# The first projections in quarters of the weights' rows, with the modulation of the next quarter between their products

## What is computed

```
mod   = silu(c) @ w_mod + b_mod          # sa, ca, ga, sm, cm, gm = split(mod, 6)
mod_c = silu(c_ctx) @ w_mod + b_mod      # only sa_c, ca_c are used
h_c = rmsnorm(ctx, w) * (1 + ca_c) + sa_c
k_c, v_c = h_c @ w_in[:, K_OFF:P_OFF]    # K_OFF 1024, P_OFF 3072
h = rmsnorm(x, w) * (1 + ca) + sa
q, k, v, u = h @ w_in[:, 0:4096]         # 1024 columns each; u goes to the pooling branch
# attention over [k; k_c], gates from w_in[:, 4096:8192], pooling of u, w_o, MLP, second block
```

## Time and profile before

| | |
|---|---|
| median of 3 runs | 2528.29 us (2527.92 to 2528.49) |
| time of the profiled execution | 2526.87 us |
| its span, first to last instruction | 2525.1 us |
| PE busy | 2384.4 us, 94% |
| DVE busy | 1372.6 us, 54% |
| ACT busy | 1120.2 us, 44% |
| mean granted TensorE clock | 0.978 |

### The profile page before, as it was taken

One profiled execution on the slowest core, in us unless ns is written; L12 is line 12 of the kernel. 1 busy time (PEld: TensorE's weight loads), 2 busy tenths in 40 slices (PEclk: granted clock), 3 DMA queues, 4 the chain that ended last, 5 costly groups with the idle time before them and its releaser, 6 DMA issues.

```text
span 2525.1 us, 31441 instructions
## 1 busy us (share of the span) xinstructions
PE 2384.4 (94%) x12376; PEld 1882.2 (75%) x12376; DVE 1372.6 (54%) x2020; ACT 1120.2 (44%) x1638; POOL 64.6 (3%) x87
## 2 busy tenths in 40 slices
PE   4699999999989998999999999999999999999998
PEld 1277887666666666888888888878888887788976
DVE  0044444666544545555555555575477555559874
ACT  2155444444433335444444444445455454456553
POOL 2000000110000000000000000000000000000000
PEclk9689999999999998999999999999999999999999
DMA  9955664666678885655655555655543566542233
GB/s 332 364 156 162 198 192 160 237 242 233 233 251 303 286 308 173 186 188 191 185 187 191 186 186 187 192 168 183 183 134 118 174 227 205 174 140 84 86 133 117
DMA packets 243187, 494.52 MB, mean 196 GB/s; under 512 B 7928, under 2 KB 8288, under 8 KB 241808
## 3 DMA queue, kind: packets, MB, share of 16 engines
q1 hardware_dynamic: 239232, 476.08, 57.0%
q0 software_dynamic: 3536, 16.94, 2.0%
q10 hardware_dynamic: 320, 0.13, 0.0%
HBM read 491.02 MB, written 2.10 MB: 195 GB/s over the span
## 4 chain that ended last, share of the span: by engine, by line
PE 69%; issue 17%; DVE 6%; DMA 6%; ACT 3%; POOL 0%; SPq 0%; ACTq 0%; DVEq 0%; POOLq 0%
PE acc L1443 18%; PE acc L1445 17%; PE acc L1444 17%; DMA raw<-in_w_mod 3%; PE acc L1749 2%; DMA raw<-in_w_in 2%; PE acc L1751 2%; PE acc L1752 2%; PE acc L1467 2%; ACT whi L487 1%; PE acc L1793 1%; PE aux L1467 1%; DVE wlo L876 1%; PE turn L1489 1%; PE turn L1807 1%
## 5 line engine op out<-in xcount | busy, mean ns | idle before, releaser
L876 DVE TENSOR_TENSOR wlo<-raw,whi 128x1024 fp32r<-128x1024 f32 x712 | 864.1, 1224 | 877.0 <-ACT whi L487 875.7
L487 ACT ACTIVATE whi<-raw 128x1024 fp32r<-128x1024 f32 x712 | 745.3, 1058 | 980.3 <-PE acc L1445 774.0
L1443 PE MATMUL acc<-whi,xhi 128*128 128x512 f32 x1792 | 713.9, 398 | 10.6 <-DVE wlo L876 4.9
L1445 PE MATMUL acc<-whi,xlo 128*128 128x512 f32 x1792 | 701.3, 391 | 0.0
L1444 PE MATMUL acc<-wlo,xhi 128*128 128x512 f32 x1792 | 701.2, 391 | 0.0
L1443 PEld LDWEIGHTS acc<-whi,xhi 128*128 128x128 f32 x1792 | 338.9, 189 | 116.2 <-issue 43.5
L1445 PEld LDWEIGHTS acc<-whi,xlo 128*128 128x128 f32 x1792 | 338.3, 189 | 72.5
L1444 PEld LDWEIGHTS acc<-wlo,xhi 128*128 128x128 f32 x1792 | 339.1, 189 | 67.3
L1443 PE MATMUL acc<-whi,hhi 128*128 128x512 f32 x512 | 201.0, 393 | 2.0 <-DVE hlo L897 2.0
L1445 PE MATMUL acc<-whi,hlo 128*128 128x512 f32 x512 | 199.4, 389 | 0.0
L1444 PE MATMUL acc<-wlo,hhi 128*128 128x512 f32 x512 | 199.3, 389 | 0.0
(11 more groups left out here) (294 smaller groups left out, 2070.0 us busy)
## 6 DMA issues: line engine op xcount, KB each, us to landing
raw<-in_w_ff SPq DMA_DIRECT2D x128, 1024.0 KB, 5.3
raw<-in_w_mod SPq DMA_DIRECT2D x96, 1024.0 KB, 5.2
raw<-in_w_in SPq DMA_DIRECT2D x80, 1024.0 KB, 5.7
raw<-in_b_w_in SPq DMA_DIRECT2D x48, 1024.0 KB, 5.1
raw<-in_a_w_in SPq DMA_DIRECT2D x36, 1024.0 KB, 5.1
raw<-in_w_o SPq DMA_DIRECT2D x16, 1024.0 KB, 7.4
raw<-in_a_w_out SPq DMA_DIRECT2D x16, 1024.0 KB, 5.0
raw<-in_b_w_out SPq DMA_DIRECT2D x16, 1024.0 KB, 5.1
```

The source lines that it names most:

```text
L487: act.activation(whi[:, k % 2, on], raw[:, n % 4, on], ACT.Copy).then_inc(hi_ready, 1)
L876: dve.tensor_tensor(wlo[:, k % 2, on], raw[:, LOAD_OF_UNIT[k] % 4, on], whi[:, k % 2, on].bitcast(F32), ALU.subtract)\
L1443: pe.matmul(bank, hi[:, kt, tok], w_hi, start=kt == k_first, stop=False, skip_group_check=True)
L1445: mm = pe.matmul(bank, lo[:, kt, tok], w_hi, start=False, stop=kt == k_first + UK * k_units - 1, skip_group_check=True)
```

## The change

The three stages `mod1`, `ctx` and `in` become one, `front`, in four passes, one for each quarter (512 rows) of `w_in`. In a pass the eight 512-column blocks come in the order u0, u1, k0, k1, q0, q1, v0, v1. Each is one unit. The k and v units are multiplied twice, by x and then by ctx, so that a pass has 12 products of one unit each, and the front 32 units in place of 48 with the same 48 products. Since a product now covers only a quarter of the sum, each is taken out of PSUM after its unit: in the first pass ACT copies it, in the other three DVE adds it to what is there.

Ahead of the first pass stand eight conditions (scale and shift of the first 512 features). The 24 others stand between the products of the first three passes: one after each of u0 and u1, two after each of k0, k1 and q0. The builds are made pass by pass (x and ctx, two each). The pooling stands after k1 and q0 of the last pass, head 0's preparation on DVE after q1 and v0.

The core of the diff:

```diff
+FRONT = [("u", 0), ("u", 1), ("k", 0), ("k", 1), ("q", 0), ("q", 1), ("v", 0), ("v", 1)]
+FRONT_CONDITIONS = (1, 1, 2, 2, 2, 0, 0, 0)
+FRONT_PRODUCTS = [(b, rows) for b, (name, _) in enumerate(FRONT) for rows in range(2 if name in "kv" else 1)]
...
+LOADS = 8 * ["mod"]
+for _quarter in range(4):
+    for _n in FRONT_CONDITIONS:
+        LOADS += ["plain"] + (_n * ["mod"] if _quarter < 3 else [])
...
+    def front_done(eng, p):
+        (quarter, n) = divmod(p, 12)
+        b, rows = FRONT_PRODUCTS[n]
+        if FRONT[b][0] in "kv" and rows == 0:
+            before = [c for c, r in FRONT_PRODUCTS[:n] if r == 0 and FRONT[c][0] in "kv"]
+            eng.wait_ge(shared_done, 4 * quarter + len(before) + 1)
+        else:
+            eng.wait_ge(units_used, 2 * (8 * quarter + b) + 2)
...
 # ScalarE
+        def take_product(p):
+            front_done(act, p)
+            act.activation(front_destination(p), banks(p), ACT.Copy).then_inc(acc_freed, 1)
+
+        copy_front_condition(0)
...
+        copy_front_condition(1)
+        front_build(0)
+        split_halves(0, 1)
+        front_build(1)
+        split_halves(1, 3)
+        for quarter in range(4):
+            for b in range(8):
+                u = 8 * quarter + b
+                products = [12 * quarter + p for p, (c, _) in enumerate(FRONT_PRODUCTS) if c == b]
+                if quarter == 0 and len(products) == 2:
+                    take_product(products[0])
+                split(u + 2, 1)
+                if quarter == 0:
+                    take_product(products[-1])
+                if b < 2:
+                    front_build(4 * quarter + 2 + b)
+                if quarter < 3:
+                    if b in (2, 4):
+                        copy_front_condition(2 * (quarter + 1) + (b == 4))
+                    if b == 6:
+                        for n in range(2):
+                            front_build(4 * (quarter + 1) + n)
...
 # VectorE
+        def add_product(p):
+            front_done(dve, p)
+            dve.wait_ge(acc_freed, p - 11)
+            dst = front_destination(p)
+            dve.tensor_tensor(dst, banks(p), dst, ALU.add).then_inc(acc_freed, 1)
...
+        for quarter in range(4):
+            for b in range(8):
+                products = [12 * quarter + p for p, (c, _) in enumerate(FRONT_PRODUCTS) if c == b]
+                if quarter and len(products) == 2:
+                    add_product(products[0])
+                split(8 * quarter + b + 2, 1)
+                if quarter:
+                    add_product(products[-1])
+                if b < 2:
+                    front_build(4 * quarter + 2 + b)
+                if quarter < 3:
+                    if b in (3, 5):
+                        take_front_condition(2 * (quarter + 1) + (b == 5))
+                    if b == 6:
+                        for n in range(2):
+                            front_build(4 * (quarter + 1) + n)
+                if quarter == 0 and b == 4:
+                    tables()
...
+                if quarter == 3 and b == 5:
+                    dve.wait_ge(acc_freed, 12 * quarter + 8)
+                    mean_squares(0, None)
+                if quarter == 3 and b == 6:
+                    prepare(0, None, RMS["att1"] + 1)
...
 # TensorE
+        for p, (quarter, (b, rows)) in enumerate((q, x) for q in range(4) for x in FRONT_PRODUCTS):
+            shared, u = FRONT[b][0] in "kv", 8 * quarter + b
+            if p >= 2:
+                pe.wait_ge(acc_freed, p - 1)
+            for part in range(2):
+                pe.wait_ge(xt_ready, 4 * quarter + 2 * rows + part + 1)
+                hi, lo, k_first = (chi, clo, 0) if rows else (xhi, xlo, 4 * quarter)
+                mm = multiply(u, 0, 1, 2 * (p % 2), k_first, hi, lo, tiles=(2 * part, 2 * part + 1), used=rows == shared)
+            if shared and rows == 0:
+                mm.then_inc(shared_done, 1)
+            if b < 2:
+                front_rows(4 * quarter + 2 + b)
+            if quarter < 3:
+                if (b, rows) == (6, 0):
+                    front_rows(4 * (quarter + 1))
+                    front_rows(4 * (quarter + 1) + 1)
+                if rows == shared:
+                    if b in (3, 5):
+                        front_columns(2 * (quarter + 1) + (b == 5))
+                    for _ in range(FRONT_CONDITIONS[b]):
+                        front_condition(next_condition)
+                        next_condition += 1
+            elif rows == shared and b in (3, 4):
...                                    # the pooling products
```

More of the change, by code:

```diff
@@ L128, in dit_kernel @@
         pass
+    with nc.sbuf_tensor("front2", [P, 12288], F32), nc.sbuf_tensor("chi", [P, 4, L], F32R) as chi, \
+            nc.sbuf_tensor("clo", [P, 4, L], F32R) as clo:
+        pass
     arena = sb("arena", [P, 16384])
@@ L543, in _ @@
[L543 to L558, removed]
@@ L559, in _ @@
-        for g in range(8):
-            build(BUILD["x"] + g, 2 * g, xhi, lambda k: scale_x[:, k:k + 1], lambda k: shift_x[:, k:k + 1])
-        u0 = UNIT["in"]
-        dst = [qk6[:, 0:2, :], qk6[:, 2:4, :], v1[:, 0:2, :], u_rows]
[L564 to L568, removed]
-            act.activation(dst[g // 2][:, :, (g % 2) * NW:(g % 2 + 1) * NW], banks(g), ACT.Copy).then_inc(acc_freed, 1)
@@ L571, in _, with copy_front_condition, front_build @@
-        for b in range(4):
-            act.wait_ge(pooled, b + 1)
-            act.activation(dT[:, 2 * b:2 * b + 2, :].rearrange("p k n -> p (k n)"), turn[:, b % 2, :], ACT.Copy)\
-               .then_inc(pooled_copied, 1)
+        def copy_front_condition(m):
+            act.wait_ge(cond_used, 4 * m + 4)
+            act.wait_ge(modcol_ready, 1 + m)
+            act.activation(modrow1, aux[:, 0, :], ACT.Copy).then_inc(modrow_ready, 1)
+        def front_build(n):
+            quarter, rows, pair = n // 4, n // 2 % 2, n % 2
+            scale, shift = ((scale_x, shift_x), (scale_ctx, shift_ctx))[rows]
+            dst = (xhi[:, 4 * quarter + 2 * pair:4 * quarter + 2 * pair + 2, :], chi[:, 2 * pair:2 * pair + 2, :])[rows]
+            act.wait_ge(turned, n + 1)
+            act.wait_ge(cond_ready, quarter + 1)
+            if n >= 2:
+                act.wait_ge(xt_ready, n - 1)
+            if rows:
+                act.wait_ge(units_used, 16 * quarter)
+            for c in range(2):
+                kt = 4 * quarter + 2 * pair + c
+                ins = act.activation(mtmp[:, n % 2, c * L:(c + 1) * L], turn[:, n % 2, c * L:(c + 1) * L], ACT.Identity,
+                                     scale=scale[:, kt:kt + 1], bias=shift[:, kt:kt + 1])
+            link(ins)
+            act.activation(dst.rearrange("p k n -> p (k n)"), mtmp[:, n % 2, :], ACT.Copy).then_inc(hi_rounded, 1)
@@ L938, in _ @@
-        ins.then_inc(cond_ready, 1)
-        for g in range(8):
-            build(BUILD["ctx"] + g, 2 * g, xhi, xlo, shift=True)
-        dve.wait_ge(params_in, 16 * SMALL)
-        for n in range(2):
-            ins = dve.tensor_tensor_reduce(out=junk[:, 0:HD], in0=lamv[:, 2 * n, :], in1=lamv[:, 2 * n + 1, :], scale=1.0,
-                                           scalar=0.0, op0=ALU.mult, op1=ALU.add, accum_out=lam[:, n:n + 1])
-            link(ins) if n == 0 else ins.then_inc(lam_sum, 1)
@@ L1446, in multiply @@
                                    skip_group_check=True)
-                if kk % 2 == 1:
+                if kk % 2 == 1 and used:
                     mm.then_inc(units_used, 1)
+            return mm
         def product(u0, g, k_units, k_first=0, hi=xhi, lo=xlo, built=None, i=None, per=0, g_count=0, g_per=0):
```

256 lines of the change are left out of this document (152 added, 104 removed).

## The result

The changed kernel takes 2532.09 us (median of 12 runs), the kernel before 2528.39 us beside it (12 runs): ratio 1.0017, with an interval of 1.001 to 1.0025. So it is slower by 0.17%, some 4 us. One of the twelve runs took 8987.62 us, and the ratios leave such runs out. The forecast was 2525 us, 3 us faster. The measured time lies in the stated range, on the other side of the time before.

What follows compares the result with a forecast made beforehand. PE bounds the kernel from the first product on. First product 54.5, PE work 309.3, waits 38.6 and low clock 12.8 end the front at 415.2; heads start at 419.5, 3 us earlier, giving 2525 us, range 2508 to 2545.

Steps and rivals of the forecast that it cites:

- first product starts: Start of the front: the first product needs 8 conditions, not 32, and starts at 54.5 us, 75 us earlier.
- k0 by ctx, three waits: PE waits for u1's banks behind the split of k1: 4.4 us a pass, 2.8 in the first.
- k1 by ctx, three waits: PE waits for k0-ctx's banks behind the split of q0: 6.15 us a pass, 4.5 in the first.
- q1, three waits: PE waits for k1-ctx's banks behind the split of q1 itself: 3.95 us a pass, 2.3 in the first.
- low clock behind the nine: PE's clock after the waits: 1.7 us for each of 4 us and more, 0.9 for 2.8, nothing for 2.3; 12.8 us.
- all other work of PE: PE's front work besides the 48 products and first low clock: transposes 6.2, conditions 27.2, columns 6.0, pooling 7.1 us.
- The landings: Unit loads in the front: k1 lands 5.2 us after the running product starts, q0, second of a pair, at 6.95.
- The end: Heads' first unit starts at 419.5 us, 3.5 plus 0.8 for low clock after PE's end; the rest only shifts.
- No waits: Rival: landing, split and addition fit under the front's products, so PE never waits; 2473 us, chance 0.08.
- Shared transfers: Rival: loads behind k1, q0 and q1 share the engines, each landing 2.75 us later, nine times; 2550 us, chance 0.10.
- A dearer clock: Rival: low clock after front waits costs 2.7 us each, not 1.7; 8 us more, 2533; an end of my case.
- my case: Three waits a pass within a microsecond each, clock between two ends; middle 2525 us, 2510 to 2540, chance 0.75.

Runs made afterwards that it cites:

- the moved program: The changed kernel with 128 idle semaphore additions at the start of TensorE's program, which move its instruction fetches: 2533.46 us, ratio 1.002.
- the kernel with the emptying first: The changed kernel with the copy or addition of a block's last product put ahead of the split two blocks on: 2488.87 us, ratio 0.9841.
- the repeat: The changed kernel as it is, run again beside the one with 128 idle semaphore additions: 2533.31 us, ratio 1.0016.
- the conditions between the products: The changed kernel with the conditions behind a k block put between its x and ctx products: 2482.04 us, ratio 0.9818.
- the one without the chain: The changed kernel with emptying and ctx builds ahead of the split, and a k block's conditions between its two products: 2466.14 us, ratio 0.9756.
- one load at a time: The changed kernel, with loads behind k1, q0 and q1 issued only when that unit has landed (passes 1 to 3): 2527.54 us, ratio 0.9999.

## Why the prediction was wrong

The mechanism held. Nine waits, three in each pass but the last, at k0 by ctx, k1 by ctx and q1, for ACT in the first pass and DVE in the next two; none at v0, v1 or in the last pass; the pooling covered. The forecast rested on a difference of 3 us between a gain of 75 and losses of nearly the same size, and several terms were a little off. The step that failed is the landing of the loads, and behind it the charge for the low clock. Set against its own ledger, in us (profiled execution; the front's products end at 420.7; forecast 415.2; "took" for a product is the time from its start to the start of what follows):

| term | forecast | measured | |
|---|---|---|---|
| first product starts | 54.5 | 51.35 | -3.1 |
| its low clock | 1.7 | 8.38 for 5.44 | +1.2 |
| k0 by ctx, three waits | 11.6 | 3.48, 5.32, 5.28 | +2.5 |
| k1 by ctx, three waits | 16.8 | 4.72, 6.54, 6.25 | +0.7 |
| q1, three waits | 10.2 | 2.46, 5.36, 6.11 | +3.7 |
| low clock behind the nine | 12.8 | 16.4 | +3.6 |
| all other work of PE (46.5) | 46.5 | 43.4 | -3.1 |

The sum is +5.5. (The waits are counted as the forecast counted them, from 5.44 behind the product's start, or 7.65 at q1; the rows' idle times are some 0.3 shorter except at q1, since the end of a matmul is modelled. "Other work" is what is left of 369.4. It is less mostly because a pair of conditions took 1.85 and not 2.21, and a single one 1.0 and not 1.22.)

*The landings* are the step that failed: "It lands at 5.2" for k1 and "it lands at 6.95" for q0 and, in the same way, q1. Counted in the same way, from the product's start, k1 landed at 5.9, 6.1 and 6.1, q0 at 7.2, 7.3 and 7.0, q1 at 7.1, 8.3 and 9.1. These excesses are the excesses of the waits, one for one; the sum of 3.0 or 4.65 behind the landing needed no correction. k1 was priced by the earlier trace rows as "A lone megabyte". That row is not a lone load, since a unit's load goes out 0.4 us behind each (731.14 and 731.56 in the earlier trace rows), and it is one of `w_mod`. The trace of before has the right row in its stage `in`, where loads of `w_in` go out 5.44 us apart (260 to 390 us, median from issue to landing):

```profile
raw<-in_w_in SPq DMA_DIRECT2D x24, 1024.0 KB, 5.4
```

So 0.3 us of k1's excess was the wrong row. Its successor made the other 0.4: with that kept back k1 landed after 5.40 and 5.54, where no instruction transfer lay beside it. Why `w_mod` lands sooner, and with a successor, no run shows.

q1's part goes with the instruction transfers: in the moved program the loads of q1 in passes 2 and 3 took 7.07 and 6.90, near the 6.95 of the forecast. I used no such row, but the trace of before has it, in the stage and the window from which the prices were read. Of the unit loads in `up` the one of 731.56 landed after 7.45 us and was taken; that of 751.56 landed after 8.31, with this beside it (751.56 to 759.87):

```profile
q8 instruction: 1, 0.02, 0.8%
```

*The clock.* "I charge 1.7 to each wait of 4 us and more" was about right in this execution: those seven products took 1.5 to 2.5 us more than 5.44. "Nothing to that of 2.3" was wrong: the wait before q1 in the first pass was 2.48 and cost 1.76, and that of 3.18 cost 1.83 and not 0.9. These two make 2.7 of the 3.6. The 1.7 was also low by the forecast's own case: the product that starts at 148.96 in the trace of before ends at 156.57, 2.2 over 5.44. The 2.15 us of idle time before the pooling without a drop, on which I rested, did not carry over. But a short wait does not always cost, either. In the kernel with the emptying first a wait of 2.05 us was followed by a clock of 1.00, and one of 2.04 by 0.69 and a product of 7.16 us (columns of the earlier trace rows, from the first matmul behind each wait):

```profile
79.08:82.06 2.98, 2.98 (x12) 2.17 (x12) 0.00 (x0) 0.13 (x1) 0.00 (x0) 1.00 0.02 5
107.38:110.36 2.98, 2.98 (x9) 2.38 (x10) 2.61 (x4) 2.83 (x4) 0.00 (x0) 0.69 1.02 359
```

The same instructions behind the same wait differ from trace to trace too. The heads' first unit, behind a wait of 2.96 us, took 7.24 here, 8.57 in the repeat of the same program, and 5.68 with the conditions between the products, at a clock of 1.00:

```profile
376.29:379.29 3.00, 3.00 (x13) 2.49 (x14) 0.00 (x0) 0.00 (x0) 0.00 (x0) 1.00 0.02 5
```

Behind the nine waits the low clock cost 16.4 here and 18.8 in the repeat, 3.6 and 6.0 over the 12.8 of the forecast, so that its share of the error is known no better than to 2 or 3 us.

*The start* went the other way. The terms of the count add up to 55.3 and not to 55.6, and the 54.5 was my choice below it. The eighth condition's group, columns and builds were through 3 us before that, but at the price of a first product of which half ran at the low clock.

*The end* held: 424.50 is 3.8 behind the end of the products (3.5 and 0.8 counted). The clock was low behind the wait of 2.96 there, as was allowed for, but it cost 1.8 and not 0.8: the heads' first unit took 7.24 and not 5.44. Behind that the programs agree: from the heads' start to the end 2102.5 us before and 2103.3 after. So 1.9 at the heads' start and 0.8 behind it make the 2.7 us of the span. From the span of 2527.8 to the median of 2532.09 are 4.3, where 3.2 was added: the profiled execution was 2 us faster than the median.

*The rivals.* No waits: false for this kernel, and right as a price for the one without the chain. Shared transfers: false. The successor did not cost 2.75 nine times, but 0.4 at k1, and q1 stayed late without it; the first of a pair landed at about 6, not 7.9. A dearer clock was the right side to look to: that rival had 8 us more, the profiled execution shows 3.6 and the repeat 6.0. The landings, 6.9 us in the waits (6.4 in the repeat), did as much or more.

*The chances.* The terms' errors were 1 to 4 us each, beside a forecast gain of 3. That was said, with 0.30 for slower and 0.28 for the same; what was wrong was to have the middle of my case as low as 2525, by taking for every landing one row of the trace, at k1 one of another matrix, and for the shortest wait no clock at all. That the miss is 7 us and not 13 is luck: the start and the other work of PE gave back 6.2.

## What to carry to other kernels

When a ring of buffers is fed by one ordered queue and emptied by engines that work in order, look for a loop: here PE's product stood behind the emptying of a bank, that behind the split of a new unit, that behind its load, and that behind a condition which PE did just ahead. Such a loop stops an engine although all engines in it are half idle; the moved lines that put the emptying ahead of the split took 43 us away, moving the conditions one product forward 50, and both together 64. And when a small difference of large terms is forecast, price a landing by rows of the same matrix and the same neighbours, all of them and not one, and give the clock behind each wait of 2 us and more a range: here it cost from nothing to 3 us.

## What was not expected of the hardware

- One instruction transfer of 16 KB beside a 1 MB load went with a landing some 1 to 2 us later (8.0 to 9.0 us against 6.8 to 7.3), in nine places of five traces, and moved with it when the places of the fetches were moved. It took 0.7% of 16 engines over 8.21 us, which is 0.9 us of one engine. In pass 2 of the changed kernel the total rate stayed what it was in pass 1 (2.86 MB in 8.21 us, 2.44 MB in 6.99 us, 348 GB/s both times), so the other engines went on with later loads meanwhile; in pass 3 it was 316 GB/s. With one load at a time the late loads ended with one or two of the 16 engines at work. So a share that ends last is seen; why it is late by more than the transfer's own 0.9 to 1.4 us, and why a few loads with such a transfer are not late, is open.
- A wait of 2.04 to 2.48 us between products was followed by a granted clock of 0.50 in some places, while it stayed at 1.00 behind 2.05 us in the same trace and behind the 2.15 us ahead of the pooling in the trace of before. In the moved program a wait of 2.58 us before q1 in pass 1 was followed by a product of 5.60 us, where the changed kernel had 2.48 and 7.20. What sets these apart was not tried.
